# Head attentions of a two-layer transformer block: two query tiles a step, turned probabilities as the stationary operand

## The reference

```
q k v = split(h @ w_in)                        # heads of 64
s     = q @ k.T (+ bias or window mask)        # 128 queries x 512 or 256 keys
p     = softmax(s)                             # window attention: one more logit, the sink
y     = p @ v
out   = concat(y) @ w_out
```

## Time and profile before

| | |
|---|---|
| median of 3 runs | 2620.39 us (2618.93 to 2620.96) |
| the profiled execution | 2621.06 us |
| its span | 2619.3 us |
| PE, PEld busy | 2505.5 us (96%), 2079.9 us (79%) |
| DVE, ACT, POOL busy | 1626.1 us (62%), 1275.3 us (49%), 253.6 us (10%) |
| mean granted TensorE clock | 0.988 |
| `block1` on PE | 147.43 to 255.84 us, next layer at 258.43 us |
| `window` on PE | 744.04 to 817.85 us, next layer at 819.73 us |

### The profile page before, as it was taken

One profiled execution on the slowest core, in us unless ns is written; L12 is line 12 of the kernel. 1 busy time (PEld: TensorE's weight loads), 2 busy tenths in 40 slices (PEclk: granted clock), 3 DMA queues, 4 the chain that ended last, 5 costly groups with the idle time before them and its releaser, 6 DMA issues.

```text
span 2619.3 us, 41629 instructions
## 1 busy us (share of the span) xinstructions
PE 2505.5 (96%) x15930; PEld 2079.9 (79%) x15930; DVE 1626.1 (62%) x2680; ACT 1275.3 (49%) x2372; POOL 253.6 (10%) x266
## 2 busy tenths in 40 slices
PE   6999999999989999999999999899999999999998
PEld 4855678889957999889886687688889899778887
DVE  2657565553688786768776863533326799775664
ACT  3356454433657765533336743422225644675554
POOL 3000100001302100315000001000002330011000
PEclk8999999999999999999999999999999999999999
DMA  7265522224555555534324534522236555634555
GB/s 282 89 227 185 193 96 96 96 88 133 159 178 194 168 180 170 174 109 150 121 97 143 159 122 171 207 96 96 92 94 172 165 178 172 204 107 143 184 173 149
DMA packets 137895, 393.58 MB, mean 150 GB/s; under 512 B 13776, under 2 KB 40400, under 8 KB 137616
## 3 DMA queue, kind: packets, MB, share of 16 engines
q1 hardware_dynamic: 135872, 386.47, 45.5%
q0 software_dynamic: 1872, 5.02, 0.7%
HBM read 390.39 MB, written 1.05 MB: 149 GB/s over the span
## 4 chain that ended last, share of the span: by engine, by line
PE 82%; DVE 8%; ACT 4%; DMA 3%; issue 2%; POOL 1%; SPq 0%; ACTq 0%; DVEq 0%; POOLq 0%
PE bank L647 21%; PE bank L649 20%; PE bank L648 20%; PE bank L644 4%; PE bank L695 3%; PE bank L854 2%; DVE w_low L1863 2%; PE bank L643 2%; PE bank L864 2%; PE bank L879 1%; ACT w_high L1163 1%; DVE smax L2130 1%; PE bank L877 1%; DMA ring<-in_w_down 1%; PE bank L835 1%
## 5 line engine op out<-in xcount | busy, mean ns | idle before, releaser
L1863 DVE TENSOR_TENSOR w_low<-ring,w_high 128x1024 fp32r<-128x1024 f32 (+2 forms) x604 | 688.1, 1141 | 523.8 <-ACT w_high L1163 520.7
L647 PE MATMUL bank<-h_high,w_high 128*128 128x512 f32 (+1 forms) x2576 | 884.2, 343 | 36.2 <-DVE h_low L2060 8.1
L649 PE MATMUL bank<-h_high,w_low 128*128 128x512 f32 (+1 forms) x2576 | 870.5, 338 | 0.0
L648 PE MATMUL bank<-h_low,w_high 128*128 128x256 f32 (+1 forms) x2432 | 821.6, 338 | 0.0
L1163 ACT CAST w_high<-ring 128x1024 fp32r<-128x1024 f32 (+2 forms) x604 | 574.5, 954 | 302.2 <-DMA ring<-in_w_down 146.8
L647 PEld LDWEIGHTS bank<-h_high,w_high 128*128 128x128 f32 x2576 | 493.8, 192 | 98.3 <-issue 24.9
L649 PEld LDWEIGHTS bank<-h_high,w_low 128*128 128x128 f32 x2576 | 493.8, 192 | 50.4
L648 PEld LDWEIGHTS bank<-h_low,w_high 128*128 128x128 f32 x2432 | 465.6, 191 | 49.4 <-issue 1.7
L647 PE MATMUL bank<-f_high,w_high 128*128 128x256 f32 (+1 forms) x616 | 194.7, 316 | 4.1 <-DVE w_low L1863 3.5
L649 PE MATMUL bank<-f_high,w_low 128*128 128x256 f32 (+1 forms) x616 | 193.0, 313 | 0.0
L648 PE MATMUL bank<-f_low,w_high 128*128 128x256 f32 (+1 forms) x528 | 168.1, 318 | 0.0
(11 more groups left out here) (285 smaller groups left out, 3495.4 us busy)
## 6 DMA issues: line engine op xcount, KB each, us to landing
ring<-in_w_up SPq DMA_DIRECT2D x176, 512.0 KB, 3.4
ring<-in_w_mod SPq DMA_DIRECT2D x112, 512.0 KB, 4.2
ring<-in_w_down SPq DMA_DIRECT2D x80, 384.0 KB, 3.1
ring<-in_w_down SPq DMA_DIRECT2D x80, 320.0 KB, 3.0
spare_slabs<-in_w_mod SPq DMA_DIRECT2D x48, 512.0 KB, 8.0
ring<-in_w_gate SPq DMA_DIRECT2D x48, 512.0 KB, 3.4
ring<-in_w_k SPq DMA_DIRECT2D x32, 512.0 KB, 3.5
ring<-in_w_v SPq DMA_DIRECT2D x32, 512.0 KB, 3.4
```

The lines of the kernel that those rows point to most:

```text
L647: pe.matmul(out, wh[:, cols], high, start=first, stop=False)
L648: pe.matmul(out, wh[:, cols], low, start=False, stop=False)
L649: ins = pe.matmul(out, wl[:, cols], high, start=False, stop=last)
L1863: v.tensor_tensor(wl[:, cols], raw[:, cols], wh[:, cols].bitcast(F32), ALU.subtract).then_inc(low_ready, 1)
```

## The change

The pair attentions get a helper of their own on each engine, `attend_heads`, over steps of two query tiles (`Heads`, `head_steps`). Where the keys are 512, a step has two "uses" of the banks, one for each tile; where they are 256, one use holds both tiles side by side. `block1` has 16 steps, eight of each kind in turn, and `window` eight.

- The value product is swapped: the turned probabilities (128 x 128) are stationary and the values (64 columns) stream, so the output comes by token.
- The probabilities are not scaled. `store` scales the output by the reciprocal sums, in four pieces of 128 x 64, into a buffer by token.
- The output is turned back by two transposes (`output_turn`), and ACT and DVE take its high and low halves straight from the bank, step by step. Values of the next step wait for the low half.
- The sinks' exponentials are one instruction of 128 x 4 for each step.
- Modulation slabs come in groups of three or four for each step, the first group ahead of the attention (`modulation_beside`).

```diff
-                    for t in range(last + 1):
-                        for i, rows in enumerate(unit["rows"]):
-                            p = probt[(sets * u + i) % len(probt)][:, t * P:(t + 1) * P]
-                                ins = pe.matmul(OUTB[rows, 0:P], unit["v"][i][t], p, start=(t == 0), stop=(t == last))
+            def scores(j):
+                    w = A.steps[j]["T"]
+                    for s, tiles in A.of(j):
+                        if s >= 2:
+                            pe.wait_ge(ex_ready, e0 + 2 * s - 2)
...
+            def output_turn(j):
+                    pe.wait_ge(o_ready, p0 + j + 1)
+                    for x in range(2):
+                        ins = pe.transpose(OUTB[:, S + x * P:S + x * P + P], TOKEN_OUT[j % 2][:, x * P:x * P + P], IDENT)
+                    ins.then_inc(o_turned, 1)
...
+            def values(j):
+                    pe.wait_ge(pt_ready, t0 + 2 * (uses[-1][0] + 1))
+                    if j:
+                        pe.wait_ge(o_halved, n["halved"] + j)
+                    for s, tiles in uses:
+                        for x in tiles:
+                            for i in range(2):
+                                at = (2 * x + i) * HD
+                                for t in range(last + 1):
+                                    b = tiles.index(x) * (last + 1) + t
+                                    ins = pe.matmul(OUTB[:, at:at + HD], HEAD_PROBT[(2 * s + i) % 8][:, b * P:(b + 1) * P],
+                                                    A.steps[j]["v"][i][t], start=(t == 0), stop=(t == last))
+                    ins.then_inc(pv_done, 1)
...
+                scores(0)
+                for j in range(A.count):
+                    if j + 1 < A.count:
+                        scores(j + 1)
+                    modulation_beside(A, A.slabs[j + 1], A.slabs[j + 2])
+                    if j >= 2:
+                        output_turn(j - 2)
+                    turn(j)
+                    if j:
+                        values(j - 1)
+                output_turn(A.count - 2)
+                values(A.count - 1)
+                output_turn(A.count - 1)
```

On ACT a step is high(j-2), copy(j), exps(j+1); on DVE it is:

```diff
+                    if j + 1 < A.count:
+                        maxima(j + 1, slice(0, 1))
+                    if j >= 2:
+                        low(j - 2)
+                    if j + 1 < A.count:
+                        maxima(j + 1, slice(1, 2))
+                    inverse_sums(j)
+                    if j:
+                        store(j - 1)
...
+                    for a in range(4):
+                        ins = v.tensor_scalar(TOKEN_OUT[j % 2][:, a * HD:(a + 1) * HD], OUTB[:, a * HD:(a + 1) * HD],
+                                              srec[:, (4 * j + a) % NS:(4 * j + a) % NS + 1], None, ALU.mult)
```

More of the change, by code:

```diff
@@ L476, in units_pair @@
                     out.append(dict(
[L477 to L482, removed]
@@ L483, in units_pair @@
-                        rows=halves, out=O[:, chunk0 + c, qt * P:(qt + 1) * P]))
-            return out
+                        subs=[[(G[rows, qchunk + c, t * P:(t + 1) * P], G[rows, kchunk + (0 if shared else c), keys])
+                               for rows in halves] for t in (qt, qt + 1)],
+                        T=count * P, sink=c if sink else None,
+                        masks=None if qt >= 2 or mask is None else [[mask(2 * c + i, t) for i in range(2)] for t in (qt, qt + 1)],
+                        v=[[VT[:, k0 + t, v0 + HD * i:v0 + HD * i + HD] for t in range(count)] for i in range(2)],
@@ new lines, in head_steps, with __init__, of, copied @@
+                        chunk=chunk0 + c, tokens=slice(qt * P, (qt + 2) * P)))
+            return out
+        class Heads:
+            def __init__(self, steps, beside, shares):
+                self.steps, self.beside, self.count = steps, beside, len(steps)
+                self.tiles, self.first, self.owner = [], [], []
+                for j, step in enumerate(steps):
+                    uses = [(0,), (1,)] if step["T"] == TOK else [(0, 1)]
+                    self.tiles.append(uses)
+                    self.first.append(len(self.owner))
+                    self.owner += [j] * len(uses)
+                self.uses = len(self.owner)
+                self.slabs = [0]
+                for n in shares:
+                    self.slabs.append(self.slabs[-1] + n)
+                self.slabs += [self.slabs[-1]] * (self.count + 2 - len(self.slabs))
+                assert self.slabs[-1] == 16 * len(beside)
+            def of(self, j):
+                return [(self.first[j] + k, xs) for k, xs in enumerate(self.tiles[j])]
+            def copied(self, j):
+                made, before = self.slabs[j + 2] // 16, self.slabs[j + 1] // 16
+                return self.beside[made - 1] if made > before else None
@@ L534, in mods_until @@
         def mods_until(units, slabs, u):
-            if slabs == 48:
-                return min(2 * u, 16 + u)
-            return min(slabs, u * slabs // (len(units) - (2 if units[0]["diff"] else 0)))
+            return min(slabs, u * slabs // (len(units) - 2))
         BRANCH_FROM = {"diff_0": 30, "diff_1": 2}
-        CHUNKS = {"block1": (4, 0), "window": (2, 0), "diff_0": (4, 0), "diff_1": (2, 0)}
+        CHUNKS = {"diff_0": (4, 0), "diff_1": (2, 0)}
         def chunk_over(name, u):
@@ L841, in attend @@
             def attend(name):
                 units, beside = ATT[name], BESIDE[name]
-                diff = units[0]["diff"]
-                sets = 1 if diff else 2
-                banks, probt = (DIFF_SCORES, PROBT) if diff else (PAIR_SCORES, PAIR_PROBT)
+                sets, banks, probt = 1, DIFF_SCORES, PROBT
                 slabs = 16 * len(beside)
@@ L897, in attend @@
                 n["turned"] += len(units) * sets
+                n["probs"] += len(units) * sets
             def chunk_ready(count=KC):
@@ L1516, in attend @@
                         begin(LIN["branch" + name[4:]], ahead)
-                    if not diff and u == len(units) - 1:
-                        begin(LIN[f"mix1_{vl}"], ahead, (0,))
                     copy(u)
@@ L1523, in attend @@
                         finish(c)
-                if beside and not diff:
-                    mod_copy(beside[-1])
                 n["sub"] += len(units) * 2
@@ L2116, in attend @@
+            def attend(name, lam):
                 units = ATT[name]
-                banks = DIFF_SCORES if units[0]["diff"] else PAIR_SCORES
+                banks = DIFF_SCORES
                 j0, u0 = n["sub"], n["unit"]
@@ L2183, in attend @@
                 n["unit"] += len(units)
-                if opens is not None:
-                    begin(LIN[opens], ahead, (1,))
                 dve.wait_ge(o_ready, n["unit"])
@@ L2251, in _ @@
                     turn_chunks(range(4, 9))
[L2252 to L2254 removed]
+                    attend_heads("window", "mix1_1")
                 def ctx_normed(g):
```

252 lines of the change are left out of this document (174 added, 78 removed).

## The result

The changed kernel takes 2667.10 us (median of 3 runs, 2665.41 to 2668.84) against 2620.39 us: ratio 1.0179, 95% interval 1.0156 to 1.0203, 46.7 us slower. The forecast was +31.4 us. The time lies inside the range of 2634 to 2672, near its upper end. The profiled execution took 2668.84 us, 47.8 more than that of before.

What follows compares the result with a forecast made beforehand. PE was taken to bound the kernel, busy for 96% of the span and 82% of the chain. Terms 31.1 + 6.5 - 4.8 - 3.1 - 0.3 - 2.4 + 5.4 - 1 = +31.4 on 2620.4 gave 2652 us, range 2634 to 2672.

Steps and rivals of the forecast that it cites:

- Value products: Value products of both attentions: loading 128 x 128 probabilities sets 0.111 us a record, +31.1 us.
- Output turns: PE in both attentions: two added transposes a step, 0.27 us over 24 steps, +6.5 us.
- Grouping: Scores on PE in both attentions: grouping two units saves 0.2 us in each of 24 steps, -4.8 us.
- Slabs: Modulation slabs on PE in both attentions: fewer, larger groups save 0.12 us for a group, -3.1 us.
- Transposes: Probability transposes on PE: 256-key steps save a start, 512-key steps wait for copies, together -0.3 us.
- Heads and tails: First and last steps of both attentions: added PE waits for exponentials, scaling and output halves, together +5.4 us.
- The clock: Head of `window`: slabs in the hole take back a third of 3.1 us lost to the lowered clock, -1 us.
- - 2.4: Ahead of both attentions: first slabs fill PE's holes of 0.66 and 1.74 us, -2.4 us.
- pace near 0.054: Value products with loads hidden: 0.054 us a record, 35 us less; 2625 us (chance 0.07) or 2615 us (0.04).
- series of load and stream: Value products: load and stream one after the other, 0.165 us a record, 34 us more, 2686 us; chance 0.05.
- the one on late exponentials: Both attentions: value loads hidden, 35 us less, but scores wait some 8 us for exponentials; 2625 us, chance 0.07.

Runs made afterwards that it cites:

- the two size experiments: The changed kernel with 128 instead of 64 value columns streaming, 2664.34 us; the changed kernel with 64 instead of 128 stationary probability columns, 2643.50 us.
- b_ahead: The kernel before with two modulation slabs moved ahead of `block1`'s first scores and four ahead of `window`'s: 2619.75 us, ratio 0.9991.

## Why the prediction was right in its sign and short in its size

- **Value products, +31.1.** Right. Measured 3.69 us in `block1`, 3.61 in `window` and 1.83 with 256 keys, so 8 x (3.69 - 2.04) + 8 x (3.61 - 2.04) + 8 x (1.83 - 1.18) = +31.0. The price came from a load seen elsewhere, and the two size experiments show that the load is its cause. The Trainium skill's advice against it (TensorEngine Tiling (Array Packing), Performance Considerations) points the right way; its factor of up to 2x is 1.6 to 1.8 here.
- **Output turns, +6.5.** 24 x 0.28 = +6.7. **Grouping**, -4.8: 1.92 for four scores as forecast. **Slabs**, -3.1: 1.84 for four.
- **Transposes, -0.3.** Mis-sized. I had a wait of 0.53 less 0.44 for a copy; it is 0.33 each time and the step's transposes take 2.32, not 2.1. With 256 keys they take 1.18, as before, not 1.02. 16 x 0.28 = **+4.5**.
- **Heads and tails, +5.4.** My sum was short here: the waits that I list for `block1` (1.2, 1.6, three of 0.9 and one of 0.95) make 6.4 us, and I took 5.7. The places were right: waits at the first two steps, for DVE's scaling and for the halves. Four scalings take 0.86 us (forecast 0.8), a turn waits 0.95 (forecast 0.9). PE's idle time at the ends is 3.3 + 4.6 us in `block1` and 7.9 + 4.0 in `window` (stretches less busy time), 19.7 where I had 16.4, of which about 1.3 is the transposes' wait. So **+7.4**.
- **The clock, -1.** This is the step that failed, in its sign. I saw half clock at one place, reckoned that slabs in the hole would relieve it, and wrote that new idle follows, without asking what the new waits would do to the clock. Added up over the low stretches, one minus the granted clock times the length is 2.6 us in `block1`'s tail, 2.4 behind it, 5.1 at the head of `window` and 6.6 in its tail: 16.7 against 4.8 before (3.1 in `window` and 1.7 behind `block1`). That is an upper bound of 12, since a part falls on waiting. Place by place, against the kernels with idle work, the changed kernel loses 12.8 us, and the kernel before 2.6 (`window` lasts 75.7 us for 74.7, and nine products behind `block1` cost 1.6): 10.2 more. By the lengthened groups alone, with the waits that they hide, the kernel before loses 4.1: 8.7 more. So **about +9 to +10**, for -1. And `b_ahead` shows that even the relief I counted on wasn't there: with slabs in the hole the clock over `window`'s first stretch stayed at 0.83.

The sum with these is 31.0 + 6.7 - 4.8 - 3.1 + 4.5 - 2.4 + 7.4 + 9 = 48.3 us, or about a microsecond more with the larger clock term; the end of `window` slipped by 48.1. Only the clock's term needs other kernels' traces, and it is the least certain.

That the time still lay inside the range is partly luck. I had allowed 3 us for the clock and it was off by 10, and nothing for the transposes, which were off by 4.8. The range held them because I added up all allowances, 19 us by their list, and the large term, the products, used none of its 4.

The rivals fell where they were placed: no pace near 0.054, no series of load and stream. But the one on late exponentials was held off by the long products alone: with values stationary again, it takes a part of what they save (a step gets 0.85 us shorter where the products save 1.5). So undoing the costliest part alone doesn't mend the change. A 512-key step in its middle saves 0.3 us by grouping (scores 0.2, slabs 0.12), and pays 0.28 for the output's turn and 0.28 for a copy's wait.

## What to carry to other kernels

In float32, price a small product by what it loads: 128 x 128 stationary costs 0.11 us a record here, whether 64 or 128 columns stream behind it, and 64 stationary columns 0.06. So of two operands, the one with 64 columns belongs on the stationary side. When a change takes the filler work out of a tail, count the waits twice, once as idle time and once for the clock behind them, and look for a granted clock below 1 in every stretch that gets such waits. Where real filler can't go there, a few idle products can hold the clock: in the changed kernel they gave back 8.8 us, in the kernel before, with a small loss to regain, nothing that could be measured. And look at the ring's order before moving real slabs.

## What the runs showed of the hardware that I had not expected

- Waits of about 1 us among small products were followed by half clock: sixteen records took 3.0 to 3.6 us instead of 1.83, and the lower clock reached some 6 us into the next layer, where PE was busy without a gap (0.60 from 280 to 286 us). Not each of them: after the first in the tail of `block1` (0.95 us, at 266.24) 32 records from 267.82 on ran at full pace, while after the first in the tail of `window` (0.95 us, at 847.59) the transposes took 1.77 and 1.94 us for 1.04. With the values stationary, the same waits in the tail of `window` (0.95 to 1.12 us) left the clock at 1.00 from 832.70 to 839.69 us, with PE busy for only 3.95 of the 6.99; and behind `block1` the same wait of 1.97 us was followed by 0.72 in the kernel before and by 1.00 in the one with slabs ahead. What tells these cases apart isn't settled, so a wait of this length is a risk and no rule.
- Products whose result nobody reads, laid in the same waits, kept the clock at 1.00 in those places in three kernels. In the fourth, a wait for a transfer that they didn't cover was followed by half clock.
- In stretches that no edit touched, the clock differed between the profiled executions (0.97 or 1.00 from 2200 to 2400 us), which is worth up to 6 us, and runs of one kernel lay up to 11 us apart: a gain of 2 to 3 us, plain in the timeline, can vanish in the runs.
